# Two heads at a time, a neighbourhood bias added by VectorE, bias tables issued by ScalarE, and another order of k tiles in a two-block transformer kernel

## What is computed

```python
def first_block(x, c, ...):
    mod = silu(c) @ w_ada + b_ada                    # six rows of 2048
    h = modulate(rms_norm(x, g_norm1), sh1, sc1)
    qa, ka, va, oa, gates, qb, kb, vb = split(h @ w_in)
    h_a = mlstm_bidirectional(qa, ka, va, gates)     # 4 heads of 256
    h_a = h_a * rsqrt(mean(h_a * h_a) + EPS) * g_head_a * sigmoid(oa)
    h_b = neighborhood_attention(qb, kb, vb, rpb)    # 8 heads of 128
    x = x + ga1 * (concat([h_a, h_b]) @ w_out)
    x = x + ga2 * conv_glu(modulate(rms_norm(x, g_norm2), sh2, sc2), ...)
    return rms_norm(x, g_final)

def second_block(x, ...):
    qa, ka, va, qb, kb, vb, ga, gb = split(rmsnorm(x, norm_mix_g) @ w_in)
    ya = sliding_window_attention(qa, ka, va, sinks) @ w_branch_a   # 16 heads of 64, 4 kv heads
    yb = stick_breaking_attention(qb, kb, vb) @ w_branch_b          # 16 heads of 64
    x = x + (sigmoid(ga) * ya + sigmoid(gb) * yb) @ w_out
    x = x + swiglu(rmsnorm(x, norm_ffn_g), w_ffn_in, w_ffn_down)
    return rmsnorm(x, norm_final_g)
```

## Time and profile before

| | |
|---|---|
| runs | 2753.75 us median of 3 (2752.24 to 2755.71) |
| profiled execution | 2754.4 us, span 2752.7 us |
| busy | PE 2623.6 us (95%), DVE 1646.8 (60%), ACT 1204.8 (44%), POOL 214.9 (8%) |
| the neighbourhood heads' product, from its first matmul to the next product's | 417.61 to 499.46 us |
| fourth input product | 1561.55 to 1830.89 us |

### The profile page before, as it was taken

How to read it: one execution, slowest core, us unless ns; L and a number is a source line. 1 busy time by engine, 2 the same in 40 slices (tenths; PEclk the granted TensorE clock), 3 DMA queues, 4 the chain that set the end, 5 groups by cost and what they waited for, 6 DMA issues and landing times.

```text
span 2752.7 us, 33428 instructions
## 1 busy us (share of the span) xinstructions
PE 2623.6 (95%) x11966; PEld 2153.2 (78%) x11966; DVE 1646.8 (60%) x1824; ACT 1204.8 (44%) x1516; POOL 214.9 (8%) x274
## 2 busy tenths in 40 slices
PE   0699999999999999999999999999999999999998
PEld 0588877778888888888888867778888888888886
DVE  8887675767676756545454474556554445454444
ACT  1243434534444444344444455554455454444443
POOL 2111114110000000000010030101000000000000
PEclk9999999999999999999999999999999999999999
DMA  9798787757767666555666634355666666666664
GB/s 396 285 362 280 254 247 196 239 198 228 250 216 248 195 190 182 181 191 191 187 206 192 183 114 146 92 164 188 200 190 185 191 188 189 190 186 191 195 193 146
DMA packets 267516, 567.39 MB, mean 206 GB/s; under 512 B 17684, under 2 KB 18044, under 8 KB 266908
## 3 DMA queue, kind: packets, MB, share of 16 engines
q1 hardware_dynamic: 247264, 494.99, 57.0%
q0 software_dynamic: 19728, 70.98, 8.4%
q10 hardware_dynamic: 428, 0.14, 0.0%
HBM read 563.94 MB, written 2.10 MB: 206 GB/s over the span
## 4 chain that ended last, share of the span: by engine, by line
PE 91%; DVE 4%; DMA 2%; issue 1%; ACT 1%; POOL 0%; ACTq 0%; DVEq 0%; POOLq 0%; SPq 0%
PE gp L1159 28%; PE gp L1161 27%; PE gp L1160 27%; DVE ada_sum L1676 2%; DMA raw<-in_w_in_dram 1%; DVE w_lo L1569 1%; PE tp L1393 1%; PE tp L1435 1%; PE tp L1182 1%; PE tp L1211 1%; DMA ada_ring<-in_w_ada_dram 1%; ACT w_hi L703 0%; PE tp L1202 0%; PE tp L1503 0%; PE tp L1514 0%
## 5 line engine op out<-in xcount | busy, mean ns | idle before, releaser
L1569 DVE TENSOR_TENSOR w_lo<-raw,w_hi 128x1024 fp32r<-128x1024 f32 x872 | 1070.2, 1230 | 874.8 <-ACT w_hi L703 872.3
L703 ACT CAST w_hi<-raw 128x1024 fp32r<-128x1024 f32 x872 | 913.3, 1051 | 1112.3 <-PE gp L1161 1041.7
L1159 PE MATMUL gp<-w_hi,h_hi 128*128 128x512 f32 x2656 | 1048.7, 395 | 9.6 <-DVE w_lo L1569 5.8
L1161 PE MATMUL gp<-w_hi,h_lo 128*128 128x512 f32 x2656 | 1035.2, 390 | 0.0
L1160 PE MATMUL gp<-w_lo,h_hi 128*128 128x512 f32 x2656 | 1035.2, 390 | 0.0
L1159 PEld LDWEIGHTS gp<-w_hi,h_hi 128*128 128x128 f32 x2656 | 499.1, 188 | 121.6 <-issue 11.4
L1161 PEld LDWEIGHTS gp<-w_hi,h_lo 128*128 128x128 f32 x2656 | 498.9, 188 | 105.6
L1160 PEld LDWEIGHTS gp<-w_lo,h_hi 128*128 128x128 f32 x2656 | 499.4, 188 | 100.9 <-issue 0.2
L1159 PE MATMUL gp<-w_hi,a_hi 128*128 128x512 f32 x704 | 274.7, 390 | 0.0
L1161 PE MATMUL gp<-w_hi,a_lo 128*128 128x512 f32 x704 | 273.9, 389 | 0.0
L1160 PE MATMUL gp<-w_lo,a_hi 128*128 128x512 f32 x704 | 273.9, 389 | 0.0
(11 more groups left out here) (271 smaller groups left out, 1434.9 us busy)
## 6 DMA issues: line engine op xcount, KB each, us to landing
raw<-in_w_in_dram SPq DMA_DIRECT2D x248, 512.0 KB, 4.4
raw<-in_w_up_dram SPq DMA_DIRECT2D x176, 512.0 KB, 4.2
raw<-in_w_ffn_in_dram SPq DMA_DIRECT2D x176, 512.0 KB, 4.3
ada_ring<-in_w_ada_dram POOLq DMA_DIRECT2D x128, 512.0 KB, 5.5
raw<-in_w_down_dram SPq DMA_DIRECT2D x88, 512.0 KB, 3.9
raw<-in_w_ffn_down_dram SPq DMA_DIRECT2D x88, 512.0 KB, 4.7
proj<-in_w_ada_dram SPq DMA_DIRECT2D x64, 512.0 KB, 7.9
raw<-in_w_out_dram SPq DMA_DIRECT2D x64, 512.0 KB, 4.7
```

Of the source, the lines that this page charges most:

```text
L703: nc.scalar.copy(w_hi[:, s], raw[:, s]).then_inc(hi_ready, 1)
L1159: mm(o, hi[:, kt0 + kt, ps], w_hi[:, s, k, :], start=n == 0, stop=False)
L1161: last = mm(o, lo[:, kt0 + kt, ps], w_hi[:, s, k, :], start=False, stop=n == g.kts - 1)
L1569: V.tensor_tensor(w_lo[:, s], raw[:, s], w_hi[:, s].bitcast(F32), ALU.subtract).then_inc(lo_ready, 1)
```

## The change

- Second block: PE computes the scores of two heads in the even steps (the 128-column matmul of both, then the longer one of both) and the outputs of two heads in the odd ones. Everything else stays per head. The waits become those of the pair, and the weights of four heads are kept (`PTS`, `AAS`) where two were.
- Neighbourhood attention: `flip` is gone. q is written with its columns reversed inside each grid row (a negative step on ScalarE's copy), the output is reversed back, and VectorE adds the bias table to the scores into SBUF before it takes the maximum. ScalarE's exponential reads SBUF.
- Bias tables: ScalarE issues their transfers, four heads in one step of `g_in_b`, the others one by one behind the exponentials. GpSimd masks the first four right after its transfers of the modulation columns.
- `g_in_o` gets the k tiles 8 to 15 first (`rot`), so `h_hi` of these tiles is free four blocks before its end. The conversion of the attention's result, the sigmoid and half of the gating move there from behind the product; the square root moves into `g_in_b`. The other half of the sigmoid reads PSUM as the drain, and `g_out` transposes the mLSTM's result in two halves (after blocks 1 and 2).
- VectorE's last drain comes before its last conversion in `g_in_b`, `g_in_o` and `g_in2a`.

The diff, cut to its core (the stick-breaking part changes like the sliding-window part):

```diff
@@ -140,7 +140,7 @@
-    g_in_o = gemm(w_in, WA // CW, col0=3 * WA)
+    g_in_o = gemm(w_in, WA // CW, col0=3 * WA, rot=WA // P // KB)
@@ -429,6 +432,8 @@
+PTS = (PT[:, 0], PT[:, 1], carve(4096, 384), carve(4096 + 384, 384))
+AAS = (AA[:, 0], AA[:, 1], gate2[:, 384:768], gate2[:, 768:1152])
@@ -602,30 +590,22 @@
-    for k in range(K1 - 1):
+    for k in range(K1):
...
-        bias(n)
-    ada_cols(K1 - 1)
+        window(n)
...
-    for n in range(4):
-        window(n)
+    window(4)
...
-    bias(4)
+    window(5)
...
-    bias(5)
-    window(4)
-    ada_gate(5)
-    bias(6)
-    window(5)
-    bias(7)
-    ada_gate(6)
...
-    ada_gate(7)
-    pool.wait_ge(na_s, HB)
+    for n in range(5, 8):
+        ada_gate(n)
+    pool.wait_ge(na_max, HB)
@@ -839,6 +831,13 @@
+        if k == ML0 + (HA - 1) * ML_H + 3:
+            for n in range(4):
+                bias(n)
+        if k == ML0 + HA * ML_H + 1:
+            act.wait_ge(ml_ms, 1)
+            nc.scalar.activation(hcol[:, 2, :], hcol[:, 1, :], ACT.Sqrt).then_inc(ml_rms, 1)
+            act.preload_act_table_set("natural_log_exp_and_others")
@@ -872,17 +871,18 @@
-            nc.scalar.mul(na_qk[:, n % 2, 0], tp[:, 0, 0:S], DB ** -0.5).then_inc(na_tq, 1)
+            nc.scalar.mul(by_row(na_qk[:, n % 2, 0]), by_row(tp[:, 0, 0:S])[:, :, ::-1], DB ** -0.5
+                          ).then_inc(na_tq, 1)
...
-            if n >= 2:
-                act.wait_ge(na_ptm, n - 1)
...
-                nc.scalar.activation(na_sc[:, n % 2, t], tp[:, 1, t * S:(t + 1) * S], ACT.Exp,
+                nc.scalar.activation(na_sc[:, n % 2, t], na_sc[:, n % 2, t], ACT.Exp,
...
+            if 4 <= n + 4 < HB:
+                bias(n + 4)
@@ -893,24 +893,39 @@
-            nc.scalar.copy(proj[:, :, QB0 + n * DB:QB0 + (n + 1) * DB],
-                           tp[:, 3, 0:S].rearrange("p (t s) -> p t s", t=2)).then_inc(na_stored, 1)
+            nc.scalar.copy(proj[:, :, QB0 + n * DB:QB0 + (n + 1) * DB].rearrange(
+                "p t (r c) -> p t r c", c=GW), by_row(tp[:, 3, 0:S])[:, :, ::-1].rearrange(
+                "p (t r) c -> p t r c", t=ST)).then_inc(na_stored, 1)
+        if k == HB + 4:
+            na_high()
+    og = proj[:, :, 3 * WA:4 * WA]
...
+        act.wait_ge(block_used, g_in_o.block0 + HB + 4)
...
-    stream(g_in_o, drain_proj(g_in_o, proj, 3 * WA), each=at(g_in_o, neighbours), nxt=g_out,
-           tail=na_high, unrolled=True)
-    act.wait_ge(ml_ms, 1)
-    nc.scalar.activation(hcol[:, 2, :], hcol[:, 1, :], ACT.Sqrt).then_inc(ml_rms, 1)
-    for t in range(ST):
-        act.wait_ge(drained[t], g_out.chunk0)
-        og = proj[:, t, 3 * WA:4 * WA]
-        nc.scalar.activation(og, og, ACT.Sigmoid).then_inc(ml_rms, 1)
+        for t in range(ST):
+            act.wait_ge(drained[t], g_in_o.chunk0 + 1)
+            nc.scalar.activation(og[:, t, 0:CW], og[:, t, 0:CW], ACT.Sigmoid).then_inc(ml_rms, 1)
+    copy_o = drain_proj(g_in_o, proj, 3 * WA)
+    def drain_o(i, e):
+        if e == 0:
+            return copy_o(i, e)
+        chunk_done(g_in_o, i, e)
+        for t in range(ST):
+            if t:
+                act.wait_ge(drained[t], g_in_o.chunk0 + 1)
+            nc.scalar.activation(og[:, t, CW:2 * CW], gp[g_in_o.bank(e)][:, t, :], ACT.Sigmoid
+                                 ).then_inc(drained[t], 1)
+    stream(g_in_o, drain_o, each=at(g_in_o, neighbours), nxt=g_out, unrolled=True)
@@ -1328,14 +1342,11 @@
-            pe.wait_ge(na_bias_ready, 2 * (n + 1))
...
-                pe.wait_ge(na_exp, 2 * n)
+                pe.wait_ge(na_max, n)
...
-                o = tp[:, 1, t * S:(t + 1) * S]
-                mm(o, flip[:, :], na_bias[:, n % 4, 2 - 2 * t:2 - 2 * t + GR, :], start=True, stop=False)
-                last = mm(o, na_qk[:, n % 2, 0, t * P:(t + 1) * P], na_qk[:, n % 2, 1, :],
-                          start=False, stop=True)
+                last = mm(tp[:, 1, t * S:(t + 1) * S], na_qk[:, n % 2, 0, t * P:(t + 1) * P],
+                          na_qk[:, n % 2, 1, :], start=True, stop=True)
@@ -1427,14 +1438,19 @@
-    def outputs(n0, h, v, w):
-        half = slice((h % 2) * DH, (h % 2 + 1) * DH)
-        if h % 2 == 0 and n0 + h:
-            pe.wait_ge(o2_out, (n0 + h) // 2)
-        mm(tp[half, 3, 0:S], proj2[:, 0, v:v + DH], w[:, 0:S], start=True, stop=False)
-        mm(tp[half, 3, P:S], proj2[:, 1, v:v + DH], w[:, S:SW_N], start=False, stop=True
-           ).then_inc(o2_mm, 1)
+    def half(h):
+        return slice((h % 2) * DH, (h % 2 + 1) * DH)
+    def outputs(n0, p, cols, ws):
+        if n0 + p:
+            pe.wait_ge(o2_out, n0 // 2 + p)
+        for u in range(2):
+            mm(tp[half(u), 3, 0:S], proj2[:, 0, cols[u]:cols[u] + DH], ws[u][:, 0:S],
+               start=True, stop=False)
+        for u in range(2):
+            mm(tp[half(u), 3, P:S], proj2[:, 1, cols[u]:cols[u] + DH], ws[u][:, S:SW_N],
+               start=False, stop=True).then_inc(o2_mm, 1)
@@ -1457,16 +1473,18 @@
-            if h < HS:
+            if h < HS and h % 2 == 0:
...
-                if h >= 2:
-                    pe.wait_ge(sw_max, h - 1)
-                half = slice((h % 2) * DH, (h % 2 + 1) * DH)
+                else:
+                    pe.wait_ge(sw_max, h)
...
-                mm(tp[:, h % 2, 0:P], Q2[half, h // 2, 0:P], K2[half, g, 0:P], start=True, stop=True)
-                mm(tp[:, h % 2, P:SW_N], Q2[half, h // 2, P:S], K2[half, g, :], start=True, stop=True
-                   ).then_inc(sw_s, 1)
+                for u in range(2):
+                    mm(tp[:, u, 0:P], Q2[half(u), h // 2, 0:P], K2[half(u), g, 0:P], start=True, stop=True)
+                for u in range(2):
+                    last = mm(tp[:, u, P:SW_N], Q2[half(u), h // 2, P:S], K2[half(u), g, :],
+                              start=True, stop=True)
+                last.then_inc(sw_s, 1)
@@ -1477,9 +1495,10 @@
-            if 0 <= h < HS:
+            if 0 <= h < HS and h % 2:
...
-                outputs(0, h, VA2 + (h // (HS // HK)) * DH, PT[:, h % 2])
+                col = VA2 + (h // (HS // HK)) * DH
+                outputs(0, h // 2, (col, col), (PTS[(h - 1) % 4], PTS[h % 4]))
@@ -1810,15 +1832,24 @@
-           nxt=g_in_o, unrolled=True)
+           nxt=g_in_o, drain_first=True, unrolled=True)
...
-            V.tensor_reduce(nst[:, n % 2, 0, :], tp[:, 1, :].rearrange("p (t s) -> p t s", t=ST),
-                            AX_X, ALU.max, negate=True).then_inc(na_max, 1)
+            dve.wait_ge(na_bias_ready, 2 * (n + 1))
+            if n >= 2:
+                dve.wait_ge(na_ptm, n - 1)
+            for t in range(ST):
+                ins = V.tensor_tensor(
+                    na_sc[:, n % 2, t].rearrange("p (r c) -> p r c", r=GR),
+                    tp[:, 1, t * S:(t + 1) * S].rearrange("p (r c) -> p r c", r=GR),
+                    na_bias[:, n % 4, 2 - 2 * t:2 - 2 * t + GR, :], ALU.add)
+            link(ins)
+            V.tensor_reduce(nst[:, n % 2, 0, :], na_sc[:, n % 2], AX_X, ALU.max, negate=True
+                            ).then_inc(na_max, 1)
@@ -1850,19 +1891,21 @@
-    stream(g_in_o, drain_proj(g_in_o, proj, 3 * WA), each=in_o_each,
-           before=at(g_in_o, neighbours_before), nxt=g_out, tail=na_low, unrolled=True)
-    dve.wait_ge(ml_rms, 1)
-    link(V.reciprocal(hcol[:, 2, :], hcol[:, 2, :]))
-    for t in range(ST):
-        dve.wait_ge(ml_rms, 2 + t)
-        for h in range(HA):
-            ht = proj[:, t, h * DA:(h + 1) * DA]
-            last = V.scalar_tensor_tensor(ht, ht, hcol[:, 2, 2 * h + t:2 * h + t + 1],
-                                          proj[:, t, 3 * WA + h * DA:3 * WA + (h + 1) * DA],
-                                          ALU.mult, ALU.mult)
-    last.then_inc(ml_out, 1)
+        if k == HB + 4 + LAG:
+            na_low()
+            dve.wait_ge(ml_rms, 1)
+            link(V.reciprocal(hcol[:, 2, :], hcol[:, 2, :]))
+            gate_heads(0, lambda t: dve.wait_ge(ml_rms, 2 + t))
+    copy_o = drain_proj(g_in_o, proj, 3 * WA)
+    def drain_o(i, e):
+        if e == 0:
+            copy_o(i, e)
+        else:
+            gate_heads(1, lambda t: dve.wait_ge(drained[t], g_out.chunk0))
+    stream(g_in_o, drain_o, each=in_o_each, before=at(g_in_o, neighbours_before), nxt=g_out,
+           drain_first=True, unrolled=True)
@@ -2031,7 +2075,8 @@
-    stream(g_in2a, scaled_drain(g_in2a, proj2, rows2), each=between, nxt=g_in2b, peel=True)
+    stream(g_in2a, scaled_drain(g_in2a, proj2, rows2), each=between, nxt=g_in2b, peel=True,
+           drain_first=True)
```

More of the change, by code:

```diff
@@ L571, in ada_mod @@
                     ada(PART2C + 4 * c_ + m, K1 + c_, 2 * D + (m + 2) * ADA_W)
-            def bias(n):
-                if n < 4:
-                    pool.wait_ge(ml_s, HA)
-                else:
-                    pool.wait_ge(na_s, n - 3)
-                for a in range(2):
-                    src = bass.AP(tensor=rpb.tensor, offset=rpb.offset + n * RR * RC
```

(53 more changed lines are left out.)

30 lines of the change are left out of this document (15 added, 15 removed).

## The result

The changed kernel takes 2712.83 us (median of 4 runs, 2709.17 to 2713.58), the kernel before on the same chip 2752.99 us (4 runs, 2751.11 to 2755.71). The ratio is 0.9851, with a 95% interval from 0.9834 to 0.9868: 40 us faster. The profiled execution took 2712.82 us, span 2711.0. The forecast was 2712, range 2703 to 2730.

A forecast was written before the change was run, and what follows sets the result against it. The prediction took the tensor engine (PE), 91% of the span, to bound the kernel. Its terms, 12.5 + 13.8 + 6.9 - 1.5 + 5.5 + 3.7 + 1.2 = 42.1 us, off 2754.4 gave 2712 us, range 2703 to 2730.

The forecast's parts named there:

- Turns: Second block: a pair of steps has four changes of matmul shape on PE in place of eight, 12.5 us saved.
- Overlap: Second block: two heads' matmuls on different halves overlap with staggered starts, 0.43 us saved 32 times, 13.8 us.
- rival (c): Second block: the two heads overlap fully, 7 us more gained, 2705 us; chance 0.10.
- (a): Second block: no overlap of the two heads, only the turns are saved, 2726 us; chance 0.25.
- (b): Second block: only scores or only outputs of the two heads overlap, 2719 us; chance 0.15.
- I take nothing for it: Second block: new waits, scores behind the maximum of head h-1 instead of h-2, have one step less; charged at nothing.
- Flips: Third input product: sixteen flip matmuls leave PE, 6.9 us gained; 1.5 us charged for VectorE's additions and ScalarE's table transfers.
- Rival (d): Third input product: becomes bound by something else, steps stay at 6.2 us, flips bring nothing, 2717 us; chance 0.10.
- Bias tables: First block: earlier masks, ending near 420.5, remove three table waits and the half clock after the stall, 5.5 us.
- covered by idle time and cost nothing: ScalarE near 379 us: eight table issues, 5.3 us in sum, and the square root fall into its idle time, costing nothing.
- rival (e): ScalarE's queue: an issue holds the engine until its transfer lands; slower from 7 us each, 2771 at 9; chance 0.04.
- k tiles and drains first: Around the third input and output products: earlier conversions remove waits of 1.5, 1.6 and 0.6 us, 3.7 us; earlier drain 1.2 us.

The follow-up runs named there:

- same_half: Changed kernel with both heads of a pair on partitions and columns 0 to 63, outputs head by head (odd heads' attention not computed): 2729.79 us, one run.
- head_order: Changed kernel with PE's order alone changed: all matmuls of the first head, then all of the second, in scores and outputs: 2708.93 us, one run.
- bias_spread: Changed kernel with ScalarE issuing the first four heads' bias tables in four successive steps, not in one: 2704.92 us, one run.
- all_three: Changed kernel with ScalarE's weight copy before its exponentials, VectorE's normalisation before the modulation sum, and first four bias tables issued over four steps: 2697.85 us, ratio 0.9801.
- pair_only: Kernel before with only the second block's pairing of heads made: 2726.56 us, ratio 0.9909.

## Why the prediction came out as it did

The total of 2712.83 against 2712 is in part luck. Held against the sum by product: the pairing brought what the forecast had, but by two errors that cancel (below). The third input product without its ends brought 8.1 us in place of 6.9 - 1.5 + 5.5 = 10.9. Its ends and the output product brought 5.9 in place of 3.7 + 1.2 = 4.9. The second input and the up product gave 1.4 us on which no term stood, and which two executions of equal code differ by as well.

**Turns.** Right in kind, a little too large: 0.74 us a stick-breaking pair against 0.81, 0.54 a sliding-window pair against 0.75, so some 10 of 12.5 us.

**Overlap.** The step that failed is "a second head can start only with the first head's second record". A group takes what one head took, 0.33 + 0.53 us, and the overlap is worth 20.1 us in place of 13.8: rival (c), to which I gave 0.10. Rivals (a) and (b) fall with `same_half`. By the Trainium skill ("TensorE: Matmul & The Clock Gate", Packing small matmuls) matmuls on other rows or columns run at once some ns apart, which the 6 to 7 ns here bear out; it also says that matmuls start strictly in the program's order. I made the staggered value from the second. In `head_order` the second head's first records start at 1599.81 us and the first head's longer matmul, which the program has ahead of them, at 1600.12; the measurement decides.

**"I take nothing for it".** This failed too. I asked only whether VectorE fits into the shorter step (it does), and not what stands behind its result in ScalarE's order. The ring through the copy costs 5.6 us. The product gained 26.2 us where the forecast had 12.5 + 13.8 = 26.3. It had 6.3 us too little for the overlap; against that stand 5.6 us for the ring, some 2 us too much for the turns and the new wait of 1.1 us at L1522, and they cancel. A further 0.67 us came from the drain in the second block, which I took at nothing.

**Flips.** Right: steady steps go from 6.23 to 5.37 us, exactly 0.86 less. VectorE's longer chain is charged about as measured: with the stall absent, the normalisation first brings 66.99 us (`bias_spread`) to 65.05 (`all_three`), so some 1.9 us were left there against my 1.5. No run takes the additions alone, so that they cause it is not shown. Rival (d) did not come.

**Bias tables.** The three waits and the old half clock went, as forecast. More than half of the 5.5 us, 3.3, came back: the masks end at 424.8, not at 420.5, since half of the sixteen selects take 1.2 to 1.8 us instead of 0.46, two of them here, beside VectorE's work:

```profile
418.85 0.46 POOL L583 TENSOR_SCALAR_AFFINE_SELECT gate<-gate 64x288 f32<-64x288 f32 x1
...
420.83 1.24 POOL L583 TENSOR_SCALAR_AFFINE_SELECT gate<-gate 64x288 f32<-64x288 f32 x1
```
```profile
420.30 4.23 DVE L1698 SCALAR_TENSOR_TENSOR ada_sum<-ada_ring,c_act,ada_sum 128x1024 f32<-128x1024 f32 x3
```

What GpSimd issues behind them is late. That is the stall of 2.3 us, with a half clock behind it; without it the third product takes 67.0 to 67.4 us instead of 70.3. And "covered by idle time and cost nothing" was wrong: an issue held ScalarE for 1.6 us on average over the eight and 3.82 at most. That is not rival (e)'s "until its transfer lands", which takes 5.1 us at least, and far from the 7 us at which (e) decides. Block 37 loses 1.8 us by it, and over the traces with the issues in one step blocks 37 to 39 lose 1.9 to 3.9. The late weight block of before, 2.8 us at block 43, is gone; in `pair_only`, with the same code there, it was 0.5 us, so what went in exchange is uncertain.

**k tiles and drains first.** The waits named are gone: the first block of the third product takes 3.08 us in place of 4.86, the last 2.72 in place of 4.41, and the output product is 2.45 us shorter. No run has this part alone, but in all ten traces with it the last block is the same and the output product takes 110.6 to 111.8 us, while `pair_only`, which lacks it, is as before (4.41 and 114.45). The up product's 0.9 us I can't assign: over the runs it lies between 500.3 and 502.3 us whatever is changed.

## What to carry to other kernels

Two f32 matmuls on different halves of the array took the time of one here, so pair them wherever a head fills only 64 rows or columns. When a step gets shorter, follow each ring of waits round all engines, in the order in which each engine has them: an instruction whose input is ready but which stands behind one that waits sets the next bound. Moving an issue to another queue also moves what is behind it, and changes what the transfer costs; on ScalarE's queue, spreading the small transfers over steps took their cost from the tensor engine. Before a difference between two single traces is put down to an edit, look at it block by block: part of it can lie in blocks that the edit does not touch.

## What the hardware showed that I had not expected

- Full overlap of f32 matmuls of two records each, in either program order: 0.86 us for the scores of two heads, 1.50 us on one half.
- Of eight issues at once on ScalarE's queue the first two took 0.70 and 0.67 us and the other six 1.9 us on average, 0.65 to 3.82; on GpSimd's the same eight took 0.65 us each.
- The transfer engines at a share of 1.01 moved 230 GB/s with the tables at once on GpSimd's queue and 334 with them spread on ScalarE's, in the same 10 us.
- A select of 64x288 on GpSimd took 0.45 us, or 1.2 to 1.8 us where VectorE worked beside it.
